# The arena of scratch buffers laid ahead of the fixed buffers in a two-block transformer kernel

## What is computed

```
first block (one layer):
    proj = x @ w_in                         # 1024 x 2560: q, k, v, gate, pool
    ret  = retention(rope(q), rope(k), v) * silu(gate);  pool = window means
    x    = layernorm(a * x + [ret, pool] @ w_out)        # 1024 x 1024
    u    = x @ w_up                         # 1024 x 5632: val, gate
    x    = layernorm(a * x + (silu(conv(gate)) * val) @ w_down)   # 2816 x 1024
second block (two layers):
    x += s5_mixer(rms(x))                   # ssm_w_in, a state-space scan, w_glu 1024 x 2048
    x += swiglu_ffn(rms(x))                 # 1024 x 5632, 2816 x 1024
    x += latent_attention(rms(x))           # 16 heads; w_kv_a has 288 columns
    x += swiglu_ffn(rms(x))                 # 1024 x 5632, 2816 x 1024
```

## Time and profile before

| | us |
|---|---|
| median of 3 runs | 1736.04 |
| lowest and highest run | 1735.53, 1739.34 |
| the profiled execution, span | 1737.8 |
| TensorE busy in it | 1713.3 (99%) |
| VectorE, ScalarE, GpSimd busy | 803.3, 665.0, 621.8 |
| clock of TensorE granted over the span | 0.996 of full speed |

### The profile page before, as it was taken

One profiled execution on the slowest core, in us unless ns is written; L12 is line 12 of the kernel. 1 busy time (PEld: TensorE's weight loads), 2 busy tenths in 40 slices (PEclk: granted clock), 3 DMA queues, 4 the chain that ended last, 5 costly groups with the idle time before them and its releaser, 6 DMA issues.

```text
span 1737.8 us, 22298 instructions
## 1 busy us (share of the span) xinstructions
PE 1713.3 (99%) x8786; PEld 1408.3 (81%) x8786; DVE 803.3 (46%) x1473; ACT 665.0 (38%) x1157; POOL 621.8 (36%) x302
## 2 busy tenths in 40 slices
PE   8999999999999999999999999999999999999999
PEld 6887888888887778789888888899767988888887
DVE  4876899586866659432111111148774311111111
ACT  3433254244244745434222212276863432122221
POOL 4433203303304223524453434434622245344342
PEclk9999999999999999999999999999999999999999
DMA  9522245443545358323333233222201233332322
GB/s 247 99 74 85 65 119 155 151 139 121 164 128 171 112 198 285 95 74 109 97 93 95 89 100 97 93 82 67 73 2 49 76 107 97 97 97 89 106 91 79
DMA packets 241895, 189.59 MB, mean 109 GB/s; under 512 B 40576, under 2 KB 198912, under 8 KB 241792
## 3 DMA queue, kind: packets, MB, share of 16 engines
q1 hardware_dynamic: 239920, 182.79, 35.4%
q10 hardware_dynamic: 1872, 5.37, 0.9%
HBM read 168.73 MB, written 19.40 MB: 108 GB/s over the span
## 4 chain that ended last, share of the span: by engine, by line
PE 89%; DVE 6%; ACT 2%; issue 2%; DMA 1%; DVEq 0%; SPq 0%; ACTq 0%
PE ps L394 14%; PE ps L396 14%; PE ps L395 14%; PE ps L422 10%; PE ps L424 10%; PE ps L423 10%; PE ps L485 3%; PE ps L487 2%; PE ps L486 2%; PE ps L938 1%; PE ps L968 1%; PE ps L510 1%; PE ps L948 1%; DVE x_rows L1864 1%; PE ps L792 0%
## 5 line engine op out<-in xcount | busy, mean ns | idle before, releaser
L1146 POOL TENSOR_TENSOR w_lo<-w_raw,w_hi 128x1024 fp32r<-128x1024 f32 (+3 forms) x246 | 573.6, 2342 | 1017.6 <-ACT w_hi L1303 1006.7
L394 PE MATMUL ps<-a_hi,w_hi 128*128 128x512 f32 (+1 forms) x1184 | 442.1, 373 | 0.0
L395 PE MATMUL ps<-a_lo,w_hi 128*128 128x512 f32 (+1 forms) x1184 | 440.4, 372 | 0.0
L396 PE MATMUL ps<-a_hi,w_lo 128*128 128x512 f32 (+1 forms) x1184 | 440.3, 372 | 0.0
L1303 ACT ACTIVATE w_hi<-w_raw 128x1024 fp32r<-128x1024 f32 (+3 forms) x283 | 282.9, 1019 | 205.8 <-DMA w_raw<-in_ffn_w_gate_up_dram 71.1
L394 PEld LDWEIGHTS ps<-a_hi,w_hi 128*128 128x128 f32 x1184 | 223.0, 188 | 40.3 <-issue 1.9
L396 PEld LDWEIGHTS ps<-a_hi,w_lo 128*128 128x128 f32 x1184 | 223.0, 188 | 38.9
L395 PEld LDWEIGHTS ps<-a_lo,w_hi 128*128 128x128 f32 x1184 | 223.0, 188 | 38.3
L2352 DVE TENSOR_TENSOR ev<-ps,xh 128x512 f32<-128x512 f32 x44 | 30.4, 691 | 411.9 <-PE ps L396 383.0
L422 PE MATMUL ps<-w_hi,h_hi 128*128 128x512 f32 x444 | 175.8, 396 | 0.0
L424 PE MATMUL ps<-w_hi,h_lo 128*128 128x512 f32 x444 | 175.2, 395 | 0.0
(11 more groups left out here) (360 smaller groups left out, 2347.9 us busy)
## 6 DMA issues: line engine op xcount, KB each, us to landing
w_raw<-in_ffn_w_gate_up_dram SPq DMA_DIRECT2D x88, 512.0 KB, 3.8
w_raw<-in_w_up_dram SPq DMA_DIRECT2D x44, 512.0 KB, 4.1
w_raw<-in_ffn_w_down_dram SPq DMA_DIRECT2D x40, 512.0 KB, 3.8
w_raw<-in_w_in_dram SPq DMA_DIRECT2D x20, 512.0 KB, 4.3
w_raw<-in_w_down_dram SPq DMA_DIRECT2D x20, 512.0 KB, 3.9
s_records<-stage SPq DMA_DIRECT2D x16, 544.0 KB, 5.3
w_raw<-in_ssm_w_glu_dram SPq DMA_DIRECT2D x16, 512.0 KB, 4.4
rec<-s_records SPq DMA_DIRECT2D x14, 544.0 KB, 5.6
```

What stands on the lines that cost most here:

```text
L394: pe.matmul(bank, wh, xh_, start=first, stop=False)
L395: pe.matmul(bank, wh, xl_, start=False, stop=False)
L396: return pe.matmul(bank, wl, xh_, start=False, stop=last)
L1146: pool.tensor_tensor(w_lo[:, n % RING, 0:w], w_raw[:, n % RING, 0:w], w_hi[:, n % RING, 0:w].bitcast(F), ALU.subtract).then_inc(lo_made, 1)
```

## The change

The arena now begins at `base`, rounded up to a multiple of 512, and has a fixed room of 99584 bytes, which holds the highest offset in use. The fixed buffers follow it, in the same order as before and without rounding.

```diff
         base = (nc.sbuf_base + 31) // 32 * 32
         KB = 1024
-        at_now = [base]
+        arena = (base + 511) // 512 * 512
+        room = 99584
+        at_now = [arena + room]
...
         eps_c = fixed("eps_c", [P, 4], F)
-        arena = (at_now[0] + 511) // 512 * 512
-        room = nc.sbuf_top - arena
+        assert at_now[0] <= nc.sbuf_top
```

## The result

The kernel with the change takes 1727.75 us (median of 4 runs, 1725.76 to 1729.21) against 1736.69 us for the kernel before (4 runs, 1735.53 to 1739.34): 0.9947 of the time, 95% interval 0.9933 to 0.9961. That is 9 us or 0.5% less; the forecast was 1727.0 us.

A forecast was written before the change was run, and what follows sets the result against it. TensorE's matmul pace was taken as the bound. Only rows of h gained: 1737.8 - 9.0 = 1728.8 us span, or 1736.0 - 9.0 = 1727.0 us median; own range 1725 to 1729, 8-in-10 range 1725 to 1762.

The forecast's parts named there:

- What bounds the kernel: Whole kernel: TensorE busy 1713.3 of 1737.8 us, so time is its matmuls' pace; longest waits 6.2 and 3.8 us.
- Everything else: Transposes, plain float32 products, VectorE, ScalarE, GpSimd and DMAs: nothing taken; at most 0.6 us either way for the input wait.
- Rows of h: 1584 matmuls with `h` stationary: 232.4 ns each would become 226.7, gaining 9.0 us; at worst 1.4 us lost.
- distance 256: Rows of h after the change: moving and stationary addresses 256 bytes apart, over 512, assumed as good as 0.
- the matmuls of 288 columns: Weight rows at distances 0, 128 and 256: mean pace 132.5 ns, nothing slow; taken as weak support for 256 being cheap.
- Columns and rows of a: 4224 matmuls of 512 columns: keep distance 0 and 226.7 ns, no change; at worst 24.1 us lost.
- strided tiles: Matmuls with every second token of `a` stationary: 2.80 us for 12, 233.3 ns each; any change would be new.
- No change: Rows of h stay at 232.4 ns, as the pattern repeats every 512 bytes or memory ends matter: 1736 us, chance 0.26.
- Slower by start: Stationary tiles beginning on a multiple of 256 are slow: rows of h 44.6 us, columns 78.1 us; chance 0.20.
- Slower by height: Stationary tiles high in memory are slow: `h` gains 9.0 us, weights and `a` lose 24.1; 1751 us, chance 0.12.
- the likeliest case: The forecast itself: rows of h reach 226.7 ns, all else unchanged; 1727.0 us, chance 0.42.

The follow-up runs named there:

- the starts exchanged: Kernel before, with the fixed buffers on a multiple of 512 and `h` 128 bytes over one: 1737.07 us, ratio 0.9996.
- the step of 96: Kernel before, with the weight ring 96 bytes further from `a` and the arena beginning 32 over a multiple of 512: 1766.32 us against 1735.61.

## Why the prediction was right

*What bounds the kernel.* Right in the main: TensorE's pace decided. Its longest wait, for the first input, is again 6.2 us, and it did not begin to wait for chunks of weights.

*Everything else* was put at nothing, and that was a little off: the wait for `prob` in the attention grew by 1.3 us in every layout that gained in full.

*Rows of h.* Right in mechanism and size. 1584 x 5.7 ns = 9.0 us was the term; the three stretches give 8.6 us. The step that was a choice, that distance 256 would behave as 0, was the open one: it rested on the matmuls of 288 columns, which do not show the cost at 128 either, as the text said. The runs confirm the choice but not that support, so the choice, made with a chance of 0.42, was in part luck. The nearness of 8.9 us between the medians to the 9.0 forecast is partly luck too, since 8.6 gained in the rows of h, 1.3 lost in that wait and the differences in granted clock add up to it; at an equal clock of 0.999 it is 8.2.

*Columns and rows of a.* Right: no change to within 0.1 ns. The other two paces that the prediction named did not move either: after the change 12 matmuls of the strided tiles take 598.53 to 601.33 us, 2.80 us as in the earlier trace rows, and 24 of 288 columns take 1144.69 to 1147.87 us, 3.18 us as in the earlier trace rows.

*The rivals.* "No change" fell in both forms: the period is 256, not 512 (rows of h at 256, twice), and the ends of the memory do not matter (128 bytes in the arena alone give the gain, 128 in the fixed buffers take it back). "Slower by start" fell twice: after the change every stationary tile stands on a multiple of 256 and none is slow, and with the starts exchanged it is the unaligned one that is. "Slower by height" fell with the change itself, whose weights and `a` lie above 132,000 at the old pace. The argument held against "slower by start", that a tile on a boundary touches fewer blocks, turned out to be beside the point. The Trainium skill, in "TensorE: Matmul & The Clock Gate", Part 2, says that loading the next tile's weights takes nothing from the running matmul's reads. The 1736.0 us that the prediction drew from it did not come: at one and the same stream of weights, shifting the stationary buffer by 128 bytes changes the pace of the stream by 5.7 ns. Whether it is the weight load's reads that do this is not shown.

*The range* was wide on the upper side, since it took in the rivals; the likeliest case's own range, 1725 to 1729, held the median.

What stays open is the cause below the distance. Two reads that walk through the same memory and meet every 256 bytes would give a table that repeats as this one does. But no run here separates the weight load from the matmul beside it, or either from what the other engines read and write, so this was only argued.

## What to carry to other kernels

When a kernel is bound by TensorE, compare the pace of one loop with different operands, from starts in the timeline, before looking for waits: a few ns per matmul are invisible in a busy share and were 9 us here. Give the moving and the stationary operands of long fp32r matmuls addresses that leave the same remainder over 256 bytes; here that is one constant in the allocator, and a stray 32 to 128 bytes ahead of the ring (in three of the four kernels with the arena moved by 32 or 96 bytes as well) cost 17 to 31 us. A layout change that moves everything should be taken apart by the smallest shift that could do the same.

## What was not expected of the hardware

The cost does not grow with the distance: 64 costs 2.2 ns over the best pace while 32 and 96 cost 6.6, and the mirror image of 64, at 192, costs 6.6 as well. This is against what was expected of the step of 96, that 192 would be 64 the other way round.

Short matmuls go the other way. In the last columns of 256 before the second network, 60 starts in a row span 7.08 us in the kernel before (120.0 ns each) and 6.94 us in the kernel with the ring 64 bytes further on (117.6 ns). Before:

```profile
797.98 0.28 PE L396 MATMUL ps<-a_hi,w_lo 128*128 128x256 f32 x1
...
805.06 0.28 PE L395 MATMUL ps<-a_lo,w_hi 128*128 128x256 f32 x1
```

With the ring 64 bytes further on:

```profile
799.99 0.28 PE L395 MATMUL ps<-a_hi,w_hi 128*128 128x256 f32 x1
...
806.93 0.28 PE L397 MATMUL ps<-a_hi,w_lo 128*128 128x256 f32 x1
```

So in the same kernel a distance of 192 costs 6.6 ns at 512 columns and gives back 2.4 ns at 256. The kernel has too few such matmuls (3 x 192) for this to pay: 1.4 us.
